# One sum of expert outputs behind each of four lo splits, in place of two behind each of two

## What is computed

```
logits = hf @ router                       # (256, 8)
top_v, top_i = top_k(logits, 2)
gates = sum(one_hot(top_i) * softmax(top_v))
y = 0
for e in range(8):
    y = y + gates[:, e] * (silu(hf @ w_gate[e]) * (hf @ w_up[e])) @ w_down[e]    # 1024 -> 2816 -> 1024
x = x + g2 * y
out = rmsnorm(x, final_gain)
```

## Time and profile before

| | us |
|---|---|
| median of 3 runs | 1738.46 |
| lowest and highest | 1735.08, 1742.9 |
| the profiled execution, its own time | 1738.31 |
| its span, first to last instruction | 1736.5 |
| mean granted TensorE clock | 0.959 of full |

### The profile page before, as it was taken

One profiled execution on the slowest core, in us unless ns is written; L12 is line 12 of the kernel. 1 busy time (PEld: TensorE's weight loads), 2 busy tenths in 40 slices (PEclk: granted clock), 3 DMA queues, 4 the chain that ended last, 5 costly groups with the idle time before them and its releaser, 6 DMA issues.

```text
span 1736.5 us, 21479 instructions
## 1 busy us (share of the span) xinstructions
PE 1592.0 (92%) x8461; PEld 1318.2 (76%) x8462; DVE 1316.7 (76%) x1445; ACT 842.8 (49%) x828; POOL 0.2 (0%) x4
## 2 busy tenths in 40 slices
PE   6989899999999897799599999999998998998994
PEld 2988787888887696467578888887886887786882
DVE  6898567767778746674568798888888888878886
ACT  6422322212212335231457777676667666756763
POOL 0000000000000000000000000000000000000000
PEclk8999999999999898699699999999999999999998
DMA  9664135443677130000479999999989898988981
GB/s 353 231 229 136 62 122 168 154 163 122 202 232 242 45 122 1 0 1 19 153 272 349 345 352 322 331 351 335 336 314 340 311 332 310 325 287 314 348 318 75
DMA packets 209452, 391.80 MB, mean 226 GB/s; under 512 B 7818, under 2 KB 82220, under 8 KB 209348
## 3 DMA queue, kind: packets, MB, share of 16 engines
q1 hardware_dynamic: 207120, 389.43, 64.5%
q10 hardware_dynamic: 2228, 0.94, 0.2%
HBM read 389.30 MB, written 1.05 MB: 225 GB/s over the span
## 4 chain that ended last, share of the span: by engine, by line
PE 78%; DVE 12%; ACT 5%; issue 3%; DMA 2%; SPq 0%; DVEq 0%; ACTq 0%
PE bank L579 19%; PE bank L581 19%; PE bank L580 19%; DVE lo L538 5%; ACT hi L532 3%; PE bank L2292 3%; PE bank L2293 3%; DVE acc L1231 2%; PE bank L2158 2%; PE bank L2147 2%; PE bank L2314 2%; PE bank L2332 1%; DVE X L1728 1%; PE bank L2333 1%; PE bank L1865 1%
## 5 line engine op out<-in xcount | busy, mean ns | idle before, releaser
L538 DVE TENSOR_TENSOR lo<-raw,hi 128x2048 fp32r<-128x2048 f32 x328 | 742.6, 2280 | 208.9 <-ACT hi L532 208.1
L532 ACT ACTIVATE hi<-raw 128x2048 fp32r<-128x2048 f32 x328 | 625.0, 1908 | 507.9 <-PE bank L581 429.7
L2292 PE MATMUL bank<-hi,xg 128*128 128x512 f32 (+1 forms) x384 | 144.5, 384 | 15.4 <-DVE lo L538 15.3
L1231 DVE SCALAR_TENSOR_TENSOR acc<-raw,cs,acc 128x512 f32<-128x512 f32 x216 | 146.6, 745 | 2.0 <-DVE acc L1231 0.4
L2293 PE MATMUL bank<-lo,xg 128*128 128x512 f32 (+1 forms) x384 | 141.5, 376 | 0.0
L579 PE MATMUL bank<-Hhi,hi 128*128 128x512 f32 x352 | 139.7, 397 | 0.0
L581 PE MATMUL bank<-Hhi,lo 128*128 128x512 f32 x352 | 138.6, 394 | 0.0
L580 PE MATMUL bank<-Hlo,hi 128*128 128x512 f32 x352 | 137.6, 391 | 0.0
L579 PE MATMUL bank<-H3h,hi 128*128 128x256 f32 x352 | 100.2, 285 | 19.7 <-DVE lo L538 19.5
L579 PE MATMUL bank<-hi,xg 128*128 128x512 f32 (+1 forms) x288 | 109.9, 382 | 3.3 <-DVE X L1728 2.3
L580 PE MATMUL bank<-lo,xg 128*128 128x512 f32 (+1 forms) x288 | 108.8, 378 | 0.0
(11 more groups left out here) (374 smaller groups left out, 3018.6 us busy)
## 6 DMA issues: line engine op xcount, KB each, us to landing
raw<-in_moe_w_gate_dram SPq DMA_DIRECT2D x88, 1024.0 KB, 5.9
raw<-in_moe_w_up_dram SPq DMA_DIRECT2D x88, 1024.0 KB, 6.7
raw<-in_moe_w_down_dram SPq DMA_DIRECT2D x88, 1024.0 KB, 6.7
raw<-in_ada_w_dram SPq DMA_DIRECT2D x48, 1024.0 KB, 5.4
raw<-in_ffn_w_gate_dram SPq DMA_DIRECT2D x11, 1024.0 KB, 5.4
raw<-in_ffn_w_up_dram SPq DMA_DIRECT2D x11, 1024.0 KB, 5.7
raw<-in_ffn_w_down_dram SPq DMA_DIRECT2D x11, 1024.0 KB, 4.9
raw<-in_ab_w_in_dram SPq DMA_DIRECT2D x6, 1024.0 KB, 8.9
```

The costliest lines, as they stand in the source:

```text
L532: nc.scalar.activation(hi[n0 % SPL][:, 0:size], raw[slot][:, 0:size], ACT.Copy).then_inc(hi_ready, 1)
L538: nc.vector.tensor_tensor(lo[n0 % SPL][:, 0:size], raw[slot][:, 0:size], hi[n0 % SPL][:, 0:size].bitcast(F32), ALU.subtract).then_inc(lo_r ...
L1231: ins = V.scalar_tensor_tensor(out=sum_, in0=w_, scalar=c_, in1=biased[:, place_, :] if h == 0 and i < 2 else sum_, op0=ALU.mult, op1=ALU.add)
L2292: T.matmul(b[:, 0:n_], xg[:, kk, 0:P], wh[:, k, :], start=(kk == 0), stop=False, skip_group_check=True)
```

## The change

The sums of the heavy expert's outputs and those of ranks 3, 5 and 6 (added while w = 4, 6 and 7 run) are placed one behind each of four lo parts. `heavy_turns` gives for hd n which quarters are added 0, 1, 2 and 3 lo parts later; for n = 0 it is as before, and where hd stands ahead of slab 20 or 23 the order is 3, 0, 1, 2. `rank_turns` gives the quarters of the light expert before by the slab that back(p) names: 1, 2, 0, 3 for slabs 3, 4, 5, 6; at w = 1 to 3, and at w = 5, where hd stands ahead of slab 5, it is as before.

```diff
+            def heavy_turns(n):
+
+                if not n:
+                    return [range(2), range(2, 4), (), ()]
+                at = {parts[0][1]: s for (_, s), parts in HEAVY_BEFORE.items() if parts[0][0] == "hd"}[n]
+                return [(o,) for o in ((3, 0, 1, 2) if at in (20, 23) else range(4))]
+
+            def rank_turns(w):
+
+                if CAPS[w] != FEW or HEAVY_BEFORE[w, 5][0][0] == "hd":
+                    return {3: range(2), 4: range(2, 4)}
+                return {3: (1,), 4: (2,), 5: (0,), 6: (3,)}
...
-                if w == "hd":
-                    heavy_add(s, range(2))
-                if back(p, 1)[0] == "hd":
-                    heavy_add(back(p, 1)[1], range(2, 4))
+                for later in range(4):
+                    kind, n = back(p, later)
+                    if kind == "hd":
+                        heavy_add(n, heavy_turns(n)[later])
...
-                    if w > 1 and s in (3, 4):
-                        add_out("moe", w - 1, gate_of(w - 1), range(2 * s - 6, 2 * s - 4))
+                    if w > 1:
+                        add_out("moe", w - 1, gate_of(w - 1), rank_turns(w).get(s, ()))
```

## The result

The changed kernel took 1747.85 us (median of 11 runs, 1738.65 to 1755.62) against 1736.15 us for the kernel before (11 runs, 1729.94 to 1742.9). The ratio is 1.0063, with a 95% interval of 1.0038 to 1.0088: slower by 11.7 us. The profiled execution of the changed kernel took 1742.42 us, with a span of 1740.6 against 1736.5.

A forecast was written before the change was run, and what follows sets the result against it. PE, busy 92% of the span, was taken as the bound, in a loop with ACT's hi and DVE's lo. Won 11.95, lost 13.6 plus 4.5 of clock: net + 6.15, so 1744.5 us, with 8 in 10 for 1737 to 1751.

The forecast's parts named there:

- my own case: Whole kernel: gains outweighed by bank waits and clock, net + 6.15 us to 1744.5 us, range 1739 to 1747; chance 0.60.
- Heavy sums, common case: Behind hd at n = 1, 3, 5, 6 and 9: third lo ends 1.32 us earlier, 6.6 us won.
- The sign that I gave for it: At hg, waits of 1.42 us would fall to 0.1 to 0.4, with a lone sum between lo's.
- n = 2: Behind hd n = 2: gathers and a transposition hold PE there, so nothing won.
- n = 10: Behind hd n = 10: DVE works without a pause to the last lo, same work, so nothing won.
- n = 7: Before slab (6,20): quarter 3 summed first ends slab (6,22)'s 3.73 us wait for bank 6; 4.75 us won.
- Light sums: At w = 4, 6 and 7: the turn of chunk 0 waits for quarter 0 in bank 4; 11.8 us lost.
- n = 8: Before slab (6,31): slab (7,2) waits for the fourth quarter's sum in bank 2; 1.8 us lost.
- The clock: Four new stalls of 3.8 to 5.5 us; three lower PE's clock at 1.5 us each, 4.5 us lost.
- third rival: Bank 4 and bank 2 stalls: low clock lasts twice as long, 3.1 us each; 1752.3 us, 0.8% slower; chance 0.15.
- "faster" rival: At the turns: bank 4 is not the hold, so the 11.8 us and their clock go; 1729.7 us; chance 0.10.
- "nothing": Light experts' stretch: ACT's hi is late anyway, gains and losses both small; 1738 to 1741 us; chance 0.15.

The follow-up runs named there:

- e8: The kernel before, sums still in pairs, but at n = 7 quarters 3 and 0 first, then 1 and 2; 1736.73 us in one run.
- e1: The changed kernel with the light sums in the order 0, 1, 2, 3 in place of 1, 2, 0, 3; 0.9957 of the kernel before.
- e7: The changed kernel with the light sums in the order 1, 2, 3, 0, so quarter 0 fourth; 1762.86 us in one run.
- e5: The changed kernel with light sums back in pairs and heavy sums also in the order 3, 0, 1, 2 at n = 8; 0.9925 of the kernel before.
- e4: The changed kernel with 14 unread matmuls keeping PE busy ahead of the turn of chunk 0 at w = 4, 6 and 7; 1.0018 of the kernel before.
- e2: The changed kernel with only the light sums moved, the heavy ones left in their old pairs; 1.0103 of the kernel before.
- e3: The changed kernel with only the heavy sums moved, the light ones left in their old pairs; 0.9957 of the kernel before.
- e10: e5 with, in six places, no heavy sum behind the first lo, one each behind second and third, two behind the fourth; 0.9902 of the kernel before.

## Why the prediction was right, and where it was short

The time lay in the range for 8 in 10 (1737 to 1751) and moved the way that was forecast, but it lay above the 1739 to 1747 of my own case, and the forecast of +0.35% lies just below the interval. The measured difference, 11.7 us, is nearly twice the forecast 6.15, and what came, slower by over 0.5%, had been given a chance of 0.18. There is some luck in the range: the kernel before took 1736.15 us in its 11 runs, 2.3 us less than the 1738.46 that I had added to; with 11.7 on top of that it would have been 1750.2, just inside. By its steps:

*Heavy sums, common case.* Right. In the changed kernel hg starts 1.3 us earlier against the slabs ahead of it at n = 1, 3, 5, 6 and 9, and 0.66 at n = 4 (0.6 forecast). The sign that I gave for it was wrong: the wait at hg fell from 1.42 to 0.77, not to 0.1 to 0.4, because the 1.32 took the 0.63 before the second slab first (0.63 + 1.42 - 1.32 = 0.73). n = 2 gave nothing, and at n = 10 what was won at slabs (7,26) and (7,27) was lost again two slabs later.

*n = 7.* Right: 4.6 us (4.75 forecast), and e8 gets it without any spreading.

*Light sums.* Right in place, cause and size: 11.8 us forecast, 11.6 in the waits. e1 removes them by the order alone, and e7 lengthens them by the forecast 8.6.

*n = 8.* Right: a wait for quarter 3 in bank 2, with a loss of 1.8 us and a fall of the clock forecast (3.3 together). Against the slabs ahead of (7,1), PE was 3.2 us later behind slab (7,3). e5 shows it as mendable.

*The clock.* **This term was mis-sized.** I took three falls of 1.5 us, 4.5 in all. The clock fell at all four stalls, and at w = 6 it stayed low about twice as long. What each turn cost beyond its wait is 5.5 - 3.7 = 1.8 at w = 4, 5.5 - 3.7 = 1.8 at w = 7 and 7.25 - 4.2 = 3.0 at w = 6 (shift of the slabs behind the turn, less the wait); with 1.4 at n = 8 (the 3.2 there less the 1.8 forecast) that is 8.0 us. That this is the clock is shown at w = 4 and w = 7 by e4, which took 1.6 us of the 1.8 away by keeping it at 1.00; at w = 6 and n = 8 it is read from the windows alone. The forecast of 6.15 plus the missing 3.5 is 9.65, against 9.2 in the stretch of the profile. The median difference of 11.7 us is not told apart from it, as the interval reaches from 6.6 to 15.3.

The third rival had this mechanism and doubled the low clock at every stall; it was right at one of the four (w = 6). In other profiles the double fall came at other stalls: in e2 at w = 4 and w = 7, in e3 at slab (7,2). Nothing in these profiles tells which stall pays twice. The "faster" rival is refuted by the changed kernel's rows at the turns, and "nothing" by e3.

All four long stalls (3.69, 4.21, 3.69 and 5.44 us) lowered the clock. The Trainium skill, "TensorE: Matmul & The Clock Gate", section "Why this matters for your kernels", had asked for that with its rule against long idle gaps, and the trace agrees. From it I had named 1746; I chose less, on a stall of 2.11 us that had not lowered it.

## What to carry to other kernels

When work is moved back in an engine's queue, write down for each bank it empties who writes that bank next and after which slab. Here two banks out of eight turned a gain of 0.75% (e5) into a loss of 0.63%, and the order inside the group mattered more than the spreading. Move work to behind the item that a long piece elsewhere hides, and put nothing ahead of the one that ends the loop: one sum in place of two ahead of the third lo was worth 0.66 us behind all six hd slabs where it was tried.

## What the runs showed of the hardware that I had not expected

The same stall lowers the clock in one execution and not in another. Before slab (4,3) PE waits 2.1 us for its lo in every kernel here: 2.11 us in the kernel before, with the clock at 1.00, and 2.10 us in e10, where it fell (PE's timeline, then a window of e10):

```profile
1192.94 0.47 PE L2305 MATMUL bank<-hi,xg 128*128 128x512 f32 x1 [2.10 <-DVE lo L538]
...
1192.00:1197.00 5.00, 4.06 (x11) 3.26 (x12) 5.00 (x3) 1.84 (x2) 0.00 (x0) 0.66 0.83 275
```

It cost e10's slabs behind it 1.6 us. The wait of 1.81 us at hg n = 7 is a second case: the clock fell behind it in e2 (0.66 over 1508 to 1513) and stayed at 1.00 in the kernel before, where the wait is as long. How long the clock stays low differs too, 0.66 over 1599 to 1604 in the changed kernel and 0.57 over 1598 to 1606 in e3: the stall of 5.44 to 5.46 us before slab (7,2) left slab (7,4) 3.2 us late in the changed kernel's profile, 3.5 in e1's, 4.0 in e3's and 4.4 in e4's, each against the slabs ahead of the stall.

Executions of one kernel differ along with this clock. Of the 11 runs of the changed kernel the shortest, 1738.65 us, had a mean granted clock of 0.961 and the longest, 1755.62, of 0.949; of the 11 runs of e3 the shortest, 1723.90, had 0.962 and the longest, 1738.68, had 0.952. That more stalls widen the spread is not shown: the changed kernel spreads over 17 us in 11 runs and e5, with no long stall, over 5 in 6 runs, but e2, with four long stalls, spreads over 7.5 us in 6 runs, and e3, with one, over 15 in 11.
